# Running the last three units of each down product tile by tile, and passing each tile's residual and norm through VectorE, ScalarE and GpSimd in turn

## What is computed

```python
h = rms_norm(x) * gain * (1 + scale) + shift     # scale, shift, gate: silu(c) @ ada_w
y = inner(h @ w_in)                              # SwiGLU, short conv, or an attention
x = x + weight * gate * rms_norm(y @ w_out)      # in the second block: x + gate * (y @ w_out)
```

| sublayers | kind | tokens in | tokens in the down product | down units | norm of y |
|---|---|---|---|---|---|
| s0, s2, s4, s6 | ffn | 256 | 256 | 11 | yes |
| s1 | short conv | 256 | 256 | 4 | yes |
| s3 | kv: shared keys and values, no down product | 256 | - | 0 | - |
| s5 | nsa attention | 256 | 256 | 4 | yes |
| s7 | differential attention | 512 | 512 | 4 | no |
| s8 | ffn | 512 | 512 | 11 | no |
| s9 | gqa attention | 512 | 256 | 4 | no |
| s10 | ffn | 256 | 256 | 11 | no |

## Time and profile before

### The profile page before, as it was taken

One profiled execution on the slowest core, in us unless ns is written; L12 is line 12 of the kernel. 1 busy time (PEld: TensorE's weight loads), 2 busy tenths in 40 slices (PEclk: granted clock), 3 DMA queues, 4 the chain that ended last, 5 costly groups with the idle time before them and its releaser, 6 DMA issues.

```text
span 2491.7 us, 34745 instructions
## 1 busy us (share of the span) xinstructions
PE 2244.0 (90%) x14158; PEld 1875.3 (75%) x14158; DVE 1202.0 (48%) x1921; ACT 959.1 (38%) x1416; POOL 14.6 (1%) x45
## 2 busy tenths in 40 slices
PE   4899897999879998777999799878999999898998
PEld 1798686898778987434897699656777768786997
DVE  0444555444624445555444565684422232665454
ACT  0433423333533335444433544464222122455333
POOL 1000000000000000000000000000000000000000
PEclk9999998999969999778999899999999999899999
DMA  7776486776437773102776522102444242222553
GB/s 284 273 277 253 169 301 222 254 255 260 163 133 256 254 262 126 51 1 85 248 259 253 127 85 85 35 1 85 153 165 155 87 167 101 76 85 77 187 176 118
DMA packets 243800, 411.37 MB, mean 165 GB/s; under 512 B 8157, under 2 KB 188854, under 8 KB 243670
## 3 DMA queue, kind: packets, MB, share of 16 engines
q1 hardware_dynamic: 243190, 408.49, 46.7%
q0 software_dynamic: 480, 1.05, 0.6%
HBM read 408.47 MB, written 1.05 MB: 164 GB/s over the span
## 4 chain that ended last, share of the span: by engine, by line
PE 76%; DVE 10%; ACT 7%; DMA 4%; issue 2%; SPq 0%; DVEq 0%; ACTq 0%
PE bank L1422 18%; PE bank L1352 13%; PE bank L1354 13%; PE bank L1353 13%; PE bank L1330 4%; PE bank L1441 2%; PE bank L1442 2%; PE bank L1443 2%; DMA stage<-in_ffn_w_out 2%; ACT gate_b L689 1%; DMA ada<-in_ada_w 1%; ACT w_hi L555 1%; PE bank L1531 1%; PE bank L1473 1%; DVE h_lo L956 1%
## 5 line engine op out<-in xcount | busy, mean ns | idle before, releaser
L879 DVE TENSOR_TENSOR w_lo<-stage,w_hi 128x2048 fp32r<-128x2048 f32 x255 | 584.4, 2292 | 763.4 <-ACT w_hi L555 763.4
L555 ACT CAST w_hi<-stage 128x2048 fp32r<-128x2048 f32 x255 | 485.3, 1903 | 748.3 <-PE bank L1422 287.2
L1352 PE MATMUL bank<-h_hi,w_hi 128*128 128x256 f32 (+1 forms) x2432 | 736.0, 303 | 1.2 <-DVE h_lo L956 1.2
L1353 PE MATMUL bank<-h_lo,w_hi 128*128 128x256 f32 (+1 forms) x2432 | 726.5, 299 | 0.0
L1354 PE MATMUL bank<-h_hi,w_lo 128*128 128x256 f32 (+1 forms) x2432 | 726.3, 299 | 0.0
L1352 PEld LDWEIGHTS bank<-h_hi,w_hi 128*128 128x128 f32 x2432 | 466.2, 192 | 62.5 <-issue 45.6
L1353 PEld LDWEIGHTS bank<-h_lo,w_hi 128*128 128x128 f32 x2432 | 466.1, 192 | 14.7 <-issue 1.2
L1354 PEld LDWEIGHTS bank<-h_hi,w_lo 128*128 128x128 f32 x2432 | 465.9, 192 | 13.8
L1422 PE MATMUL bank<-w_hi,h_hi 128*128 128x512 f32 x776 | 242.8, 394 | 13.8 <-DVE h_lo L888 11.7
L1422 PE MATMUL bank<-w_hi,h_lo 128*128 128x512 f32 x776 | 240.8, 392 | 0.0
L1422 PE MATMUL bank<-w_lo,h_hi 128*128 128x512 f32 x776 | 240.4, 391 | 0.0
(11 more groups left out here) (192 smaller groups left out, 2007.4 us busy)
## 6 DMA issues: line engine op xcount, KB each, us to landing
ada<-in_ada_w SPq DMA_DIRECT2D x120, 1024.0 KB, 7.0
stage<-in_ffn_w_in SPq DMA_DIRECT2D x88, 1024.0 KB, 6.4
stage<-in_ffn_w_out SPq DMA_DIRECT2D x44, 1024.0 KB, 4.9
stage<-in_ffn_w_gu SPq DMA_DIRECT2D x44, 1024.0 KB, 5.1
stage<-in_ffn_w_down SPq DMA_DIRECT2D x22, 1024.0 KB, 4.9
stage<-in_a_w_in SPq DMA_DIRECT2D x12, 1024.0 KB, 7.8
stage<-in_diff_w_in SPq DMA_DIRECT2D x12, 1024.0 KB, 5.1
ada<-in_kv_ada_w SPq DMA_DIRECT2D x8, 1024.0 KB, 8.3
```

Of the source, the lines that this page charges most:

```text
L555: a.copy(w_hi[:, s, :], stage[:, s, :]).then_inc(hi_done, 1)
L879: v.tensor_tensor(w_lo[:, s, :], stage[:, s, :], w_hi[:, s, :].bitcast(F32), ALU.subtract).then_inc(lo_done, 1)
L1352: m.matmul(dst[:, 0:T], wh, h_hi[:, k * T:(k + 1) * T], start=(k == 0), stop=False)
L1353: m.matmul(dst[:, 0:T], wh, h_lo[:, k * T:(k + 1) * T], start=False, stop=False)
```

## The change

- **Down.** In the last three units PE runs tile by tile: for each tile all three units, then the next tile. All three must be ready while the first tile runs, and all three are given back only while the last one runs. Behind all but the last unit of tile t (behind the first half of the columns, for the last tile), PE transposes tile t-1 of the next sublayer (`turn`); the last tile's transposes stand behind the product. For s7, tiles 2 and 3 (context) are transposed within tile 0.
- **Residual and norm** (`boundary`). In halves of 512 columns: gate times y no longer waits for the norm, whose factor comes in with the addition to x; half of `xn` is made by DVE, half by ACT. With 256 tokens, gain, scale and shift, hi and lo are done per tile of 128; with 512, per pair of tiles.
- **Who does what.** lo of the activations moves from DVE to GpSimd, which does it before it issues the tables of the same sublayer.
- **Order.** `split(nu)` stands behind the last tile but one (its hi parts on ACT, its affine steps on DVE) and ahead of the last tile's squares and residual. `split(nu+1)` stands behind everything. The first `vec_acc` of a sublayer stands behind the first half of its first product.
- **s4** takes its h from the transposes of s3: DVE, ACT and GpSimd make it during the first two units of s3, in a part of `h_hi` of its own, and its own norm, transposes and hand-over go.
- **Output** leaves in two transfers, one per tile, each released by DVE.

The core of the diff (names and offsets of buffers left out):

```diff
-            sp.wait_ge(act_s, t.at("finished"))
-            sp.dma_start(out[0].rearrange("(t p) d -> p t d", p=P), xs[:, 0:2, :]).then_inc(stored, 16)
-            sp.wait_ge(stored, 16)
+            for tt in range(2):
+                sp.wait_ge(dve_s, t.at(x_mark(len(subs), tt)))
+                sp.dma_start(out[0, tt * P:(tt + 1) * P, :], xs[:, tt, :]).then_inc(stored, 16)
+            sp.wait_ge(stored, 32)
...
+            def lo(s, k, tt):
+                tag = f"s{s['n']}"
+                pool.wait_ge(dve_s, t.at((tag, "h32", k, tt)))
+                pool.wait_ge(act_s, t.at((tag, "hi", k, tt)))
+                if s["T"] == 256:
+                    src, n = h32(k), 1
+                else:
+                    src, n = h32_pair(k), 2
...
+                t.done(g.tensor_tensor(dst, src, hi, ALU.subtract), pool_s, (tag, "lo", k, tt))
+
             for s in subs:
+                if s["T"] == 256:
+                    for tt in range(2):
+                        for k in range(KC):
+                            lo(s, k, tt)
+                else:
+                    for c in s["cs"]:
+                        for k in s["ks"]:
+                            lo(s, k, c)
...
+                    y_stats(prev, tt)
+                    if s and s["T"] == 512 and tt == n_prev - 1:
+                        act.wait_ge(w_used, nu)
+                        for k in s["ks"][5 if n_prev == 2 else 0:]:
+                            hi_pair(s, k, s["cs"][0])
+                    if s and tt in tiles:
+                        x_norm(prev, s, tt)
+                    if s and s["T"] == 256 and tt in tiles:
+                        for k in s["ks"]:
+                            hi(s, k, tt)
+                    if s and tt == n_prev - 2:
+                        if s["T"] == 512 and n_prev == 2:
+                            for k in s["ks"][0:5]:
+                                hi_pair(s, k, s["cs"][0])
+                        split(nu)
+                if s and s["T"] == 512 and n_prev:
+                    for k in s["ks"]:
+                        hi_pair(s, k, s["cs"][1])
+                if s and n_prev:
+                    split(nu + 1)
...
                     split(u + n + AHEAD)
+                    if n < 2 and s["n"] + 1 < len(subs):
+                        for k in range(KC):
+                            hi(subs[s["n"] + 1], k, n)
...
+            def y_update(s, tt):
+
+                tag, T = f"s{s['n']}", s["Td"]
+                dve.wait_ge(act_s, t.at((tag, "gateb", T // 256 - 1, 1)))
+                for h in range(2):
+                    if s["post"]:
+                        dve.wait_ge(act_s, t.at((tag, "ss", tt, h)))
+                    else:
+                        wait_y(dve, s, tag, tt, h)
+                    g = gate_b[:, tt // 2, h * 512:(h + 1) * 512]
+                    if tt:
+                        dve.wait_ge(dve_s, t.at((tag, "x", tt - 1, h)))
+                    t.done(v.tensor_tensor(upd(h), y_bank(T, tt, h)[:, :], g, ALU.mult), dve_s, (tag, "upd", tt, h))
+                    if s["post"] and h == 0:
+                        mean(0, tt, (tag, "ss", tt, 0), (tag, "mean0", tt))
+                if s["post"]:
+                    inverse(0, tt, (tag, "root", tt), (tag, "yrstd", tt))
+                for h in range(2):
+                    x = xs[:, tt, h * 512:(h + 1) * 512]
+                    dve.wait_ge(dve_s, t.at((tag, "upd", tt, h)))
+                    if s["post"]:
+                        t.done(v.scalar_tensor_tensor(out=x, in0=upd(h), scalar=st(0, tt, 4), in1=x, op0=ALU.mult, op1=ALU.add),
+                               dve_s, (tag, "x", tt, h))
+                    else:
+                        t.done(v.tensor_tensor(x, upd(h), x, ALU.add), dve_s, (tag, "x", tt, h))
+
+            def x_norm(s, tt):
+
+                tag = f"s{s['n']}"
+                mean(1, tt, (tag, "xss", tt, 0), (tag, "xmean0", tt))
+                inverse(1, tt, (tag, "xroot", tt), (tag, "rstd", tt))
+                t.done(v.tensor_scalar(xn(tt)[:, 0:512], xs[:, tt, 0:512], st(1, tt, 4), None, ALU.mult), dve_s, (tag, "xn", tt))
...
+                    y_update(prev, tt)
+                    if s and tt in tiles:
+                        x_norm(s, tt)
+                    if s and s["T"] == 256 and tt in tiles:
+                        for k in s["ks"]:
+                            affine(s, k, tt, f"s{s['n']}")
+                    if s and s["T"] == 512:
+                        if n_prev == 2 and tt == 0:
+                            for k in s["ks"]:
+                                affine_pair(s, k, s["cs"][0])
+                        if n_prev == 4 and tt in (1, 2):
+                            for k in s["ks"][4 * tt - 4:4 * tt]:
+                                affine_pair(s, k, s["cs"][0])
+                    if s and tt == n_prev - 2:
+                        split(nu)
+                if s and s["T"] == 512:
+                    for k in s["ks"]:
+                        affine_pair(s, k, s["cs"][1])
+                if s and n_prev:
+                    split(nu + 1)
...
+                    if n < 2 and s["n"] + 1 < len(subs):
+                        for k in range(KC):
+                            affine(subs[s["n"] + 1], k, n, tag)
...
+            def turn(s, tt):
+
+                tag = f"s{s['n']}"
+                for h in range(2):
+                    pe.wait_ge(*((act_s, t.at((tag, "xnb", tt))) if h else (dve_s, t.at((tag, "xn", tt)))))
+                    for k in range(4 * h, 4 * h + 4):
+                        ins = m.transpose(xt(tt, k), xn(tt)[:, k * P:(k + 1) * P], ident[:, :])
+                    t.done(ins, pe_s, (tag, "tr", tt, h))
...
+                for tt in range(n_tiles):
+                    for j in range(nb - 3, nb):
+                        if tt == 0:
+                            ready(j)
+                        if tt == n_tiles - 1 and j == nb - 1:
+                            products(j, None, tt, (0, 1), ((0,),))
+                            after(tt)
+                            ins = products(j, None, tt, (0, 1), ((1,),))
+                        else:
+                            if j == nb - 1:
+                                after(tt)
+                            ins = products(j, None, tt)
+                        if tt == n_tiles - 1:
+                            ins.then_inc(w_used, 1)
...
+                    if q == 0 and s["n"] + 1 < len(subs):
+                        pe.wait_ge(pool_s, t.at(lo_mark(subs[s["n"] + 1], KC - 1)))
...
+                            up_step(j, i, 2, (0, 2), first,
+                                    {(0, 0): (lambda: vec_acc(s["v"], 0),)} if first and s["nvec"] else None)
...
+                def after(tt):
+                    if nxt is None:
+                        return
+                    if tt:
+                        turn(nxt, tt - 1)
+                    elif nxt["T"] // P > n_tiles:
+                        for k in range(n_tiles, nxt["T"] // P):
+                            turn(nxt, k)
+
+                down(s, tag, s["v"] + 4 if early and s["nvec"] else None, after)
+                if nxt:
+                    turn(nxt, n_tiles - 1)
```

## The result

The changed kernel took **2541.1 us** (median of four runs, 2537.0 to 2544.6) where the kernel before took 2494.3: a ratio of **1.0184**, 95% interval [1.0166, 1.0201]. That is 46.8 us slower. Forecast were 2505 and a range of 2483 to 2523: the direction was right, the size was not, and the time lies 18 us above the range. The profiled execution has a span of 2537.6 us (before 2491.7), a mean granted clock of 0.930 (0.945), and TensorE is again the chain in 76 hundredths.

What follows compares the result with a forecast made beforehand. PE bounds the kernel, its largest wait being for the next sublayer's xn. Terms 15.2 - 6.6 - 2.2 + 4.1 - 0.5 - 1.0 + 0 = +9.0 on 2496.3 give 2505 us, range 2483 to 2523.

Steps and rivals of the forecast that it cites:

- Step 1: First tile of the last three units: PE waits for the second unit's h_lo, 2.15 us (2.75 at 512 tokens).
- Steps 2 and 3: 256-token hand-over: tile 0's 5.2 us chain hides within 6.8; its transposes take 1.04 per 8.
- Step 4: Before the last tile, unit nu's weight split keeps DVE until 24.8, though y lay there since 19.6: 5.2 us.
- The rival that had it out of the way: Split of nu finishes before the last tile's y, PE idles under 5 us: 2462 to 2475; chance 0.09.
- Step 5: Last tile's residual and norm at 256 tokens end at 29.15; PE idle 9.7 us, clock down as before.
- Step 6: After the last tile's norm: transposes, affine, hi, lo; first product starts at 31.3, ends at 35.8, condition vector at 37.65.
- s3 and s4: Affine steps among s3's evictions cost +1.8, the hand-over dropped at its end gives -8.4: together -6.6 us.
- Tables: Tables issued behind GpSimd's lo: in s9 there at 58.2, +4.1 us; in s7 at 45 to 53.
- 6.5 us to win at s6-s7: At s6-s7, forecast -0.5 us, up to -7 if the tables land early.
- s7-s8: 512-token hand-over: stall 2.75, but condition vector done at 55.5 against 57.7 before: -2.2 us.
- s0: Start, with no down product before it: half-wide squares and the vector behind the product, -1.0 us.
- Slow GpSimd: A 128-column subtraction costs 1.0 us instead of 0.45, so lo paces first products: about +28, 2525; chance 0.10.

Runs made afterwards that it cites:

- The experiment on its place: Changed kernel with ScalarE making w_hi of the next sublayer's first unit ahead of tile 0's h_hi copies at six 256-token hand-overs: 2528.6 us.
- The 20.5 us of the experiment: Changed kernel with s7 and s9 table DMAs issued ahead of GpSimd's h_lo subtractions, once tile 0 of the new x is there: 2520.6 us.
- the combined kernel: Changed kernel with h parts before w parts in down loops, tables in the empty stretch, next sublayer's first w split off VectorE: 2463.3 us.

## Why the prediction was wrong, step by step

- **Step 1, the stall: right, and mis-priced; this is the step that failed.** 2.30 to 2.36 us (forecast 2.15) at 256 tokens, 2.84 to 2.89 (2.75) at 512, at ten tails. The sum took the wait alone. What it drags behind it, a granted clock of 0.50 for 3 us of full work, was in the earlier trace rows for the long idle time and was not asked of the short one; the term was put at nothing without a reason. It measured 1.5 to 1.7 us at eight of the ten tails and 0.1 at the last two, 13 us in all, and the stalls themselves were 1.6 longer than forecast. With the stall mended 32 us came back.
- **Steps 2 and 3: right.** Tile 0's `xn` lies ready (PE waits only at s6-s7, 0.32 us, for a context tile), transposes take 1.03 to 1.04.
- **Step 4: right.** `w_lo` of unit nu ends at 302.3, 5.2 us after the last y (297.04). The experiment on its place confirms it: idle 10.0 to 7.7. The rival that had it out of the way falls.
- **Step 5: right**: 10.0 us idle, forecast 9.7.
- **Step 6: short by 0.3 to 1.6.** First product 2.64 us after the transposes began, not 2.15. At s0-s1, s2-s3 and s4-s5 it was slow nearly to its end, at the other three it turned fast sooner: it ended 8.1 or 7.0 to 7.2 us after those transposes began, forecast 6.65; about 5 us over the six. GpSimd's h_lo steps by 0.42 (taken 0.45) and 0.70 (taken 0.70); the upper end for the pair, by three streams of 0.22 us, is 0.85 and not 0.82. By the factor in the Trainium skill (GPSIMD Engine Reference, section 3.1) the prediction had estimated the pair near 0.7: the trace agrees, eight pairs in s9 take 5.62 us.
- **s3 and s4: right** (-4.0 with s2-s3, forecast -4.8).
- **Tables: mechanism right, short by 9.5 us; the second step that failed.** In s9 they were there at t = 63.5, forecast 58.2: lo ended at 53.3, not 51.05, and the last table landed 10.2 us behind it, not 7.2. It took 8.1 us from issue to landing beside a weight unit in flight; in the kernel before, with none in flight, it took the 5.0 of the earlier trace rows. In s7 the tables were there at t = 57, past the 45 to 53 of the forecast: lo ended at 39.9, not 37.4, and the eight transfers took 17.0 us from the first issue to the last landing. The first transposes of the heads came at t = 73.9 in s9 (68.6 by the forecast) and 71.2 in s7 (67). The 20.5 us of the experiment are another thing: they are all that the tables' wait was worth, and the forecast itself had 6.5 us to win at s6-s7 if they landed early.
- **Slow landing in s7 isn't the weights' doing.** The last of the eight took 12.3 us to land in the changed kernel, but also 11.0 in the kernel before, where no weight unit was in flight.
- **s7-s8: too hopeful by 3.** Half of it is the stall's clock (1.5 us lost); the rest stays open.
- **s0: wrong sign.** 16 subtractions take 6.7 us, and TensorE waits 2.71 us for the first of tile 1, with the condition matmuls no longer there as cover, at clock 0.50: +2.3 where -1.0 was forecast.
- **Rivals.** Slow GpSimd (2525) came nearest in time, by chance: its cause is refuted, since a subtraction steps by 0.42 us and not by 1.0. The range was built from single mechanisms around +9; no case in it let two terms be short at once, and that is why it ended at 2523. That the kernel got slower was no luck: the stall, the split in the last tile's way and the late tables were all forecast.

Added up as an estimate (10 us of slow matmuls outside the two stretches with tables, 9.5 for the tables, 5 for step 6, 3.3 for s0, 1.6 for the stalls, 2 for the idle time, 0.8 for s3 and s4) these are some 32 of the 37 us by which the traced span missed the forecast. The rest stays open.

## What to carry to other kernels

When work is cut finer to start a chain sooner, check each producer's order against the new, shorter interval: here the splits were in the right order for 5.4 us per unit and in the wrong one for 2.7. Price a stall of a full TensorE with the slow time that can follow it, not with the wait line alone: here 1.5 to 1.7 us more at eight of ten stalls of 2.3 to 2.9 us. A transfer issued by an engine moves with that engine's queue, and what matters is not only when its result is needed but what else is on the DMA engines at that moment.

## What the runs showed of the hardware

- Behind eight of the ten gaps of 2.3 to 2.9 us in full TensorE work the granted clock went to 0.50, between 0.6 us before and 1.5 us after work resumed, stayed there for some 3 us, and the matmuls lost 1.5 to 1.7 us. Behind the last two, of 2.35 and 2.30 us, it stayed at 1.00; what sets these two apart no run shows. Without the gap the same matmuls ran at 1.00. A pair of matmuls behind the first gap and behind the ninth:

```profile
281.85 1.05 PE L1527 MATMUL bank<-w_hi,h_lo 128*128 128x512 f32 x2
```
```profile
2314.18 0.62 PE L1527 MATMUL bank<-w_hi,h_lo 128*128 128x512 f32 x2
```

- An instruction of VectorE with both inputs in SBUF was held for 3.7 us while GpSimd ran one with both inputs in SBUF; its affine steps, which read PSUM, were not: eight of them beside the same GpSimd instruction took 2.64 us in the combined kernel, as without it. The Trainium skill (SBUF — State Buffer, section "SBUF: two separate sides") says that the two engines share one pair of ports as an exclusive lock, held for a whole instruction, when VectorE's has two SBUF inputs and GpSimd's reads SBUF. The trace agrees: 3.97 us, ending 0.15 us behind GpSimd's 4.53.
- Eight small tables (0.5 MB) among weights made two weight units take 21 us to land instead of 9. With no weight unit in flight the last of the eight still took 11.0 us (kernel before), and the last of the four of s9 5.0.
